# Prompt attention of a hybrid decoder step: the next item's scores behind the first turned piece of this item

## The reference, cut to what matters

```
s = einsum('btghd,bsgd->btghs', q, wk)
p = masked_softmax(s, wvalid)
o_win = einsum('btghs,bsgd->btghd', p, wv)
...
o_nsa = gates[:, :, 0] * o_cmp + gates[:, :, 1] * o_slc + gates[:, :, 2] * o_win
```

## Time and profile before

| what | value |
|---|---|
| time, median of 3 runs | 2266.75 us (2266.01 to 2271.41) |
| profiled execution, own time | 2266.64 us |
| profiled execution, span | 2265.0 us |
| PE busy, whole span | 2130.3 us (94%) |
| DVE, ACT, POOL busy | 931.0, 447.6, 544.3 us |
| mean granted clock of PE | 0.971 |
| attention stage, 597 to 897 us: PE, DVE, ACT busy | 261.05, 174.98, 147.97 us |

### The profile page before, as it was taken

One profiled execution on the slowest core, in us unless ns is written; L12 is line 12 of the kernel. 1 busy time (PEld: TensorE's weight loads), 2 busy tenths in 40 slices (PEclk: granted clock), 3 DMA queues, 4 the chain that ended last, 5 costly groups with the idle time before them and its releaser, 6 DMA issues. The chain is left out here.

```text
span 2265.0 us, 32090 instructions
## 1 busy us (share of the span) xinstructions
PE 2130.3 (94%) x12018; PEld 1748.4 (77%) x12018; DVE 931.0 (41%) x1810; ACT 447.6 (20%) x983; POOL 544.3 (24%) x525
## 2 busy tenths in 40 slices
PE   5999999899788888999999999899999999999996
PEld 5978887676465556888888778688888888888885
DVE  4352114662455656321212457533333333534544
ACT  1530001422355544100000133201101010000002
POOL 5031220023411113412111564222222322000121
PEclk9999999987899999999999999999999999999998
DMA  9621213566300000112120442111111111122422
GB/s 258 179 93 38 56 38 90 156 158 178 105 1 1 1 1 20 38 29 56 28 56 19 119 119 83 38 38 55 37 37 48 45 37 37 52 91 88 154 89 91
DMA packets 244765, 161.60 MB, mean 71 GB/s; under 512 B 34659, under 2 KB 234885, under 8 KB 244590
## 3 DMA queue, kind: packets, MB, share of 16 engines
q1 hardware_dynamic: 229500, 138.85, 22.1%
q0 software_dynamic: 5008, 18.45, 2.4%
q10 hardware_dynamic: 10146, 2.80, 0.7%
HBM read 147.52 MB, written 16.71 MB: 73 GB/s over the span
## 5 line engine op out<-in xcount | busy, mean ns | idle before, releaser
L3336 DVE TENSOR_TENSOR big<-big,ps 128x264 f32<-128x264 f32 x308 | 131.8, 429 | 352.8 <-PE ps L2996 351.3
L2996 PE MATMUL ps<-hT,ring 128*128 128x264 f32 x1056 | 251.4, 388 | 10.6 <-ACT hT L3138 10.6
L3623 PE MATMUL ps<-big,ring 128*128 128x264 f32 x1056 | 240.6, 388 | 2.5 <-PEq L3851 2.5
L2996 PEld LDWEIGHTS ps<-hT,ring 128*128 128x128 f32 x1056 | 201.8, 191 | 45.8 <-ACT hT L3138 11.1
L3623 PEld LDWEIGHTS ps<-big,ring 128*128 128x128 f32 x1056 | 201.7, 191 | 37.6 <-issue 2.8
L2996 PE MATMUL ps<-big,ring 128*128 128x264 f32 x928 | 223.1, 389 | 4.3 <-PEq L3851 4.3
L210 PE MATMUL ps<-hT,ring 128*128 128x264 f32 x912 | 213.8, 392 | 3.9 <-PEq L3851 2.5
L210 PEld LDWEIGHTS ps<-hT,ring 128*128 128x128 f32 x912 | 175.8, 193 | 36.5 <-issue 4.1
L2996 PEld LDWEIGHTS ps<-big,ring 128*128 128x128 f32 x928 | 176.3, 191 | 34.5 <-issue 4.7
L210 PE MATMUL ps<-big,ring 128*128 128x264 f32 x816 | 184.7, 386 | 0.0
L210 PEld LDWEIGHTS ps<-big,ring 128*128 128x128 f32 x816 | 155.0, 190 | 26.5
(11 more groups left out here) (473 smaller groups left out, 2941.5 us busy)
## 6 DMA issues: line engine op xcount, KB each, us to landing
ring<-in_w_ada SPq DMA_DIRECT2D x44, 512.0 KB, 5.7
ring<-in_w_in SPq DMA_DIRECT2D x34, 512.0 KB, 5.0
ring<-in_w_ff_down SPq DMA_DIRECT2D x16, 1024.0 KB, 4.9
ring<-in_w_ff_gate SPq DMA_DIRECT2D x22, 512.0 KB, 4.0
ring<-in_w_ff_up SPq DMA_DIRECT2D x22, 512.0 KB, 5.2
ring<-in_w_out SPq DMA_DIRECT2D x16, 512.0 KB, 5.3
ring<-in_w_ff_down SPq DMA_DIRECT2D x8, 768.0 KB, 4.2
x_kept<-big SPq DMA_DIRECT2D x2, 2112.0 KB, 7.4
```

Source lines behind the costliest of these rows:

```text
L2996: ins = pe.matmul(ps[:, b, 0:NH], w[:, k, :], cols[:, k, :], start=k == 0, stop=k == 3)
L3336: dve.tensor_tensor(to, x, ps[:, bank[j], 0:NH], ALU.add).then_inc(f_joined, 1)
L3623: ins = pe.matmul(ps[:, bank(n, j), 0:NH], w[:, k, :], cols[:, k, :], start=c == 0 and k == 0, stop=c == 2 and k == h - 1)
```

## The change

In PE's loop over `turned` the scores of `ahead[x + 1]` are no longer issued at the head of item x, but behind the turning of the item's first piece. The factors of a group that has just closed therefore come first in the item, directly ahead of that piece. DVE, ACT, POOL and SP keep their instructions and order. No instruction is added or removed.

```diff
             for x, y in enumerate(turned):
-                for z in ahead[x + 1]:
-                    score(z)
                 if x and closes(turned[x - 1]):
                     factors(group(turned[x - 1]))
                 for p in of_item[y]:
                     turn(p)
+                    if p == of_item[y][0]:
+                        for z in ahead[x + 1]:
+                            score(z)
                     if last is not None:
                         value(last)
                     last = p
```

## The result

The changed kernel takes 2292.99 us (median of 4 runs, 2291.73 to 2295.26), the kernel before 2266.38 in the same comparison: a ratio of 1.0118, 95% interval 1.0093 to 1.0143, so 1.2% slower. Forecast were 2281.1 and a range of 2272 to 2292. The sign and the stage were right; the loss was 26.6 us where 14.5 were forecast. Single executions of one kernel scatter together with the clock (the kernel before took 2253.6 to 2276.1 us over all comparisons, at mean granted clocks of 0.979 to 0.965, the shortest ones at the highest clock), so the number of clock falls in a profile is that of one execution.

What follows compares the result with a forecast made beforehand. PE, busy 94% of the span, was taken as the bound. 0.55 - 0.1 + 1.2 + 1.2 = 2.9 a head pair, 11.4 for four, plus 1.5 makes 12.9; 2266.64 + 12.9 + 1.6 (clock) = 2281.1 us, range 2272 to 2292.

Steps and rivals of the forecast that it cites:

- The ring into the pause: Score to next score at the item behind a closed group: 5.30 us, where it was 4.17 or 4.18.
- narrow 2: Branch 2, from the score of tile 0 to that of tile 4: +1.2 us a head pair, between 0 and 1.9.
- the head change: From a head pair's first score to its tile 4 score in branch 1: +1.2 us, between 0 and 1.9.
- the wide rings: Score-to-score times of wide items (two pieces) in branches 1 and 2; an ordinary 5-tile one 4.43 us against 4.34.
- the start: The first head pair's way to the score of tile 4: another 1 to 2 us, 1.5 taken.
- the number of clock falls: At eight new PE pauses between factors and turns: one fall to 1.2 GHz more than before, costing 1.6 us.
- wide 1: From the score of branch 1's tile 4 to branch 2's tile 0: 21.43 to 21.98 us, +0.55 a head pair.
- wide 2: From branch 2's tile 4 score to the next head pair's first score: 18.70 to 18.59 us, -0.1.
- bare ring: A 5-tile wide item's score, maxima, exponentials and next score, without ACT's copies holding back the exponentials: 4.01 us.
- The rival with eight falls: Clock falls at most of the new pauses behind the factors: 8 x 1.6 = 12.8 us, so 2292; chance 0.22.
- the clock rival: Clock falls at most new pauses between factors and turns, 12.8 us in place of 1.6: 2292 us; chance 0.22.
- The rival of filled waits: PE's waits around scores and factors get filled with work: up to 13.0 us gone, 2253.6 us; chance 0.08.

Runs made afterwards that it cites:

- the two halves: Two runs of the changed kernel: new order for wide items alone (2269.84 us against 2269.42, 0.9999), or for narrow and branch-0 items alone (2290.8 us, 1.0100).
- factors first: Kernel before, with a closed group's factors moved to the head of the item, then scores, then turns: 2257.23 us, 0.9940.
- split turns: Changed kernel, but in wide items the next score stands between the first piece's turns of group 0 and group 1: 2284.52 us, 1.0091.
- factors three times: Changed kernel with the four factor transposes of query tiles 0 to 3 issued three times: 2287.34 us, 1.0075.
- entry undone: Changed kernel, but the last narrow item of each branch (query tile 3) keeps its scores ahead of its turns: 2278.18 us, 1.0056.
- only wide items: Changed kernel, but narrow items and the branch-0 item keep the old order: 2269.84 us against 2269.42, 0.9999.
- the run on the start: Changed kernel, but the first four items of the first head pair keep the old order: 2290.31 us, 1.0111.

## Why the prediction was right or wrong

**Right**: the sign; the stage; that scores would wait no more and turns would wait for exponentials and, in half of the factors' places, some 1.8 us for their copy (19.8 us in all, 1.78 the one shown). The ring into the pause was forecast at 5.30 and is 5.33. The stretches with narrow items were forecast at +1.2 each; `narrow 2` has +1.05, and the head change +1.35 where the clock did not fall before, together the forecast 2.4 of a head pair. That the order of the narrow items makes most of the loss was shown by running the two halves.

**Wrong** were the sizes of three terms of the sum, all too small: the wide rings, the start and the number of clock falls. In the stage 14.5 us were forecast (12.9 and 1.6 for the clock), 22.8 came:

- *The wide rings.* Forecast +0.55 for `wide 1` and -0.1 for `wide 2`; measured +1.4 and, at full clock (19.08), +0.4. The bare ring of 4.01 took the turn of group 1 to start 0.95 behind the last exponentials' start, as scores did; a waiting PE starts it 1.02 behind, the exponentials come 0.79 apart, and the turn holds the score 0.45: 4.58 and not 4.43. Each further tile added 0.59 (4.58 to 5.17, 5.86 to 6.45), where 0.55 was taken although the rows gave up to 0.69. The ring of 7 key tiles (5.86) has 0.10 more, a slip of the sum: the first piece of such an item has four tiles and not three (its group-1 turn holds the score for 0.55). Over four head pairs that is 3.5 us in branch 1 and some 1.7 in branch 2.
- *The start.* Forecast 1.5 and the 1.2 of a head change, measured 4.65: 2 us more. The step that the text left out is that the stage begins at 1.2 GHz, and that with a slower start the clock stays low for longer: 19.7 us after the first score in place of 12.6. In the profiles of all runs it was 12.6 to 12.9 us with the old order at the start and 19.3 to 21.1 with the new one.
- *The clock at the pauses.* One fall more was forecast. There were four, one in each head pair at the second branch's factors, and the two at head changes were gone: 4 x 1.5 - 2 x 1.55 = 2.9 against 1.6. The rival with eight falls named the right mechanism; half of the pauses brought one. That the time came out at that rival's 2292 is chance: it had 11.2 us more from falls, where the falls gave 1.3 more.
- Smaller and of either sign: the narrow stretches at equal clock gave 0.6 less in branch 2 and 0.5 more at the head changes.
- The rest of the difference of the two profiles, 2.3 us, lies outside the stage's scores; 1.8 of it comes ahead of the stage, where the programs are the same, and the profiles scatter by more than that.

So the mechanism stood but for the low clock at the start, and the forecast's own bounds would have reached the time; the range was drawn up to the clock rival, as if the other terms had no upper ends of their own. The rival of filled waits fell for the change as it is, but it is what factors first does: the piece of the change that moved the factors ahead is worth some 12 us (2269.4 to 2257.2) if the score stays between them and the turns.

## What to carry to other kernels

In an engine that takes its work in order, ask of every pair what ends the wait of each: put the instruction first whose result goes out on the longest way (here the score, which DVE and ACT need), and put a step that has to wait for a copy of its predecessor (here the turn behind the factors) as far behind it as other work reaches. A part of a change can gain while the whole costs: run the parts. When several terms of a sum are uncertain to the same side, the range must allow for several of their upper ends, not only for the likeliest rival's.

## What the runs showed of the hardware

A pause of PE of 1.78 us between two groups of transposes was followed by a granted clock of 0.50, that is 1.2 GHz (741.9 to 745.3 in the second head pair), but only at one of two pauses of equal length in each head pair of the changed kernel (behind branch 2's, 666.8, 741.9, 816.9 and 892.0, all 75.1 apart). The place alone does not decide: with the old order at the start one of branch 1's pauses brought a fall as well (704.7), and with the split turns two (703.0 and 853.2). In the profiles of these three kernels 13 of 23 pauses of 1.78 or 1.79 brought a fall within 1.5 us of their end; of 25 pauses of 0.90 or 0.91 at the same place (factors three times, entry undone, only wide items, and one in the run on the start) none did. What tells the pauses of equal length apart stays open. And useless transposes in that pause, on no one's path, shortened the stage by 6.2 us.
